# Ranking of a routed mixture: search rounds with four candidates, list slots marked and turned by small products, row maxima over 512 keys

## The reference, cut to what matters

```python
def block(q_blk):                                        # attention, 8 heads, 2560 keys for the 2048 sample queries
    s = (jnp.einsum('bqhd,bkhd->bhqk', q_blk[..., :QK_NOPE], k_nope)
         + jnp.einsum('bqhr,bkr->bhqk', q_blk[..., QK_NOPE:], kpe))
    p = jax.nn.softmax(s.astype(jnp.float32) * scale, axis=-1).astype(v.dtype)
...
cap = EC_FACTOR * n // N_EXPERTS                         # 256 of the 2048 sample tokens for each expert
aff = jax.nn.softmax((h @ w_router).astype(jnp.float32), axis=-1)
vals, idx = lax.top_k(aff.transpose(0, 2, 1), cap)
xg = jax.vmap(lambda hb, ib: hb[ib])(h, idx)
```

## Time and profile before

| | us |
|---|---|
| median of 3 runs | 3122.05 |
| lowest, highest | 3120.58, 3127.84 |
| the profiled execution | 3117.55 |
| its span in the trace | 3115.5 |

### The profile page before, as it was taken

How to read it: one execution, slowest core, us unless ns; L and a number is a source line. 1 busy time by engine, 2 the same in 40 slices (tenths; PEclk the granted TensorE clock), 3 DMA queues, 4 the chain that set the end, 5 groups by cost and what they waited for, 6 DMA issues and landing times. The chain is left out here.

```text
span 3115.5 us, 43716 instructions
## 1 busy us (share of the span) xinstructions
PE 2905.0 (93%) x16781; PEld 2331.0 (75%) x16781; DVE 2019.8 (65%) x2589; ACT 1087.0 (35%) x1722; POOL 1065.6 (34%) x686
## 2 busy tenths in 40 slices
PE   6999999999789999999999999989948999999993
PEld 3888888888667777777777767878827888888882
DVE  5418292829357888878888865555684566666655
ACT  5311111111344444444444443223413333333344
POOL 1000000000123334444334546411107666656652
PEclk8999999999889999999999999999968999999996
DMA  6213222211541110110111136575415676666667
GB/s 231 100 53 107 78 104 81 105 66 54 183 141 24 27 31 14 27 34 13 25 27 33 34 124 197 186 251 172 144 72 174 197 203 192 194 198 200 198 188 286
DMA packets 139666, 371.48 MB, mean 119 GB/s; under 512 B 20902, under 2 KB 48012, under 8 KB 129260
## 3 DMA queue, kind: packets, MB, share of 16 engines
q1 hardware_dynamic: 100028, 266.74, 25.7%
q0 software_dynamic: 23920, 74.70, 8.9%
q10 hardware_dynamic: 15552, 27.79, 2.5%
HBM read 266.25 MB, written 102.89 MB: 118 GB/s over the span
## 5 line engine op out<-in xcount | busy, mean ns | idle before, releaser
L1176 ACT ACTIVATE at_w<-banks 128x512 f32<-128x512 f32 (+1 forms) x592 | 347.6, 591 | 467.0 <-PE banks L1282 410.9
L1398 DVE TENSOR_REDUCE at_mpart<-banks 128x2 f32<-128x512 f32 x584 | 374.0, 683 | 140.1 <-PE banks L1309 139.9
L1254 POOL TENSOR_TENSOR at_part<-at_part,at_w 128x512 f32<-128x512 f32 x224 | 297.1, 1326 | 330.7 <-ACT at_w L1176 327.4
L2601 POOL TENSOR_TENSOR moe_gu_lo<-raw,moe_gu_hi 128x2048 fp32r<-128x2048 f32 x63 | 295.6, 4703 | 91.0 <-ACT moe_gu_hi L2669 90.7
L517 DVE SCALAR_TENSOR_TENSOR fr_r<-fr_r,fr_dw 128x2334 f32<-128x2334 f32 x120 | 318.0, 2650 | 3.9
L374 PE MATMUL fr_po<-hT_hi,fr_w_hi 128*128 128x512 f32 (+1 forms) x800 | 297.1, 371 | 3.1 <-PE fr_po L374 1.9
L374 PE MATMUL fr_po<-hT_hi,fr_w_lo 128*128 128x512 f32 (+1 forms) x800 | 294.7, 368 | 0.0
L374 PE MATMUL fr_po<-hT_lo,fr_w_hi 128*128 128x512 f32 (+1 forms) x800 | 294.6, 368 | 0.0
L1321 PE MATMUL banks<-at_w,V 128*64 128x256 f32 (+1 forms) x2368 | 283.0, 381 | 0.0
L2791 DVE TENSOR_TENSOR moe_d_lo<-moe_raw_d,moe_d_hi 128x1024 fp32r<-128x1024 f32 x64 | 200.7, 3136 | 102.8 <-ACT moe_d_hi L2701 97.5
L1425 DVE TENSOR_TENSOR at_part<-at_part,at_w 128x512 f32<-128x512 f32 x224 | 231.8, 1035 | 13.0
(11 more groups left out here) (406 smaller groups left out, 6833.0 us busy)
## 6 DMA issues: line engine op xcount, KB each, us to landing
raw<-w_gate_up SPq DMA_DIRECT2D x64, 1024.0 KB
moe_raw_d<-w_down SPq DMA_DIRECT2D x64, 512.0 KB
fr_wm<-w_ada_rows POOLq DMA_DIRECT2D x32, 512.0 KB, 4.6
gates_scratch<-fr_r ACTq DMA_DIRECT2D x64, 256.0 KB, 2.0
mx_gates<-gates_scratch SPq DMA_DIRECT2D x64, 256.0 KB, 3.4
fr_raw<-w_in SPq DMA_DIRECT2D x28, 512.0 KB, 5.2
fr_r<-x POOLq DMA_DIRECT2D x18, 512.0 KB, 5.6
raw<-mixed_scratch SPq DMA_DIRECT2D x9, 1024.0 KB, 6.0
```

What stands on the lines that cost most here:

```text
L1176: act.activation(w[:, g % NW, k, 0:n], sc[:, (2 * g + k) % SCB, 0:n], ACT.Exp, scale=SM_SCALE).then_inc(exp_done, 1)
L1254: pool.tensor_tensor(part[:, j % 2, 1, 0:n], before, w[:, g % NW, 1, 0:n], ALU.add).then_inc(add_p, 1)
L1398: dve.tensor_reduce(mpart[:, s, 2 * half:2 * half + 2, c], max_bank(m, half), AX.X, ALU.max).then_inc(red_done, 1)
L2601: pool.tensor_tensor(gu_lo[:, slot], raw_gu[:, slot], gu_hi[:, slot].bitcast(F32), ALU.subtract).then_inc(glo_done, 1)
```

## The change

**Attention.** For the steps that come in pairs (all but the ninth of a sample block and the prompt's), `max_products` makes two products of 128 queries by 512 keys instead of four by 256. The even step takes query tiles 0 and 1, the odd one tiles 2 and 3, each with the keys of both steps; a bank then holds one query tile. `mpart` shrinks from 9 to 5 columns.

**Search round.** There are four candidates, the first being the bits found so far, whose count is a constant 64 per row. The new `low` is the largest candidate that is reached: compare and multiply in one instruction, a maximum over four, and one instruction that joins the next bits to it. `digit`, `kept` and the separate update of `low` go.

**Tail.** Both threshold comparisons run one behind the other and one reduction counts them. DVE writes for each list its end, and a row of 256 marks in bfloat16, 1 where the slot is at or behind that end (`past`, four instructions). PE turns and sums these by small products: per quarter two slot halves, each with `stride_b` (how far the next list lies) and with `less` (minus what the list gave). `diag`, `offs`, `places`, `begins`, `begun` go. Constants: `rank_slot`, `rank_ones` and `rank_lists` give way to `rank_stride` and `rank_slots`; ACT converts the slot numbers to bfloat16 ahead of the copy that completes `listed`.

```diff
+        def paired(m):
+            _, b, c = STEPS[m]
+            return b < NB and c < NS - 1
+
+        def max_unit(m, half):
+            _, b, c = STEPS[m]
+            first = 2 * (c % 2) + half if paired(m) else 2 * half
+            tiles = 1 if paired(m) else 2
+            k0 = key_tiles(b, c - c % 2) * P
+            bank = bank_of(("unit", UNITS[m] + half)).rearrange("p (q n) -> p q n", q=tiles)
+            return bank, slice(first, first + tiles), slice(k0, k0 + BLK // tiles)
...
-                    pe.wait_ge(hi_piece, PIECES * h + (PIECES if h else pieces(b, c)))
+                    pe.wait_ge(hi_piece, PIECES * h + (PIECES if h else pieces(b, c + 1 - c % 2 if paired(m) else c)))
...
-                        for i in range(2):
-                            at = tok + (2 * half + i) * P
-                            mm = pe.matmul(max_bank(m, half)[:, i, :], q_hi[u][0:HQ, at:at + P], k_hi[u][0:HQ, k0:k0 + 256],
-                                           start=True, stop=True)
+                        bank, tiles, keys = max_unit(m, half)
+                        for i in range(tiles.stop - tiles.start):
+                            at = tok + (tiles.start + i) * P
+                            mm = pe.matmul(bank[:, i, :], q_hi[u][0:HQ, at:at + P], k_hi[u][0:HQ, keys], start=True, stop=True)
...
-                        dve.tensor_reduce(mpart[:, s, 2 * half:2 * half + 2, c], max_bank(m, half), AX.X, ALU.max
-                                          ).then_inc(red_done, 1)
+                        bank, tiles, _ = max_unit(m, half)
+                        dve.tensor_reduce(mpart[:, s, tiles, c // 2], bank, AX.X, ALU.max).then_inc(red_done, 1)
...
+                act.wait_ge(slots_ld, 16)
+                act.activation(slots_b, slots, ACT.Copy).then_inc(same_done, 1)
                 act.wait_ge(max_done, QUARTERS * LIST // 8)
                 act.activation(listed[:, :, :, 1], val[:], ACT.Copy).then_inc(listed_done, 1)
...
                     dve.wait_ge(total_done, r + 1)
-                    dve.tensor_scalar(reach[:], total, float(CAP), None, ALU.is_ge, ALU.add, accum_out=digit[:]).then_inc(digit_done, 1)
-                    dve.wait_ge(digit_done, r + 1)
-                    wait(dve, low_done, r + 1)
-                    dve.tensor_scalar(kept[:], digit[:], float(4 ** (ROUNDS - 1 - r)), None, ALU.mult).then_inc(kept_done, 1)
-                    dve.wait_ge(kept_done, r + 1)
+                    dve.scalar_tensor_tensor(out=reach[:], in0=total, scalar=float(CAP), in1=cand[:].bitcast(F32),
+                                             op0=ALU.is_ge, op1=ALU.mult).then_inc(reach_done, 1)
+                    dve.wait_ge(reach_done, r + 1)
+                    dve.tensor_reduce(low[:], reach[:], AX.X, ALU.max).then_inc(low_done, 1)
+                    dve.wait_ge(low_done, r + 1)
                     if r + 1 < ROUNDS:
-                        dve.scalar_tensor_tensor(out=cand[:], in0=bits[:, r + 1], scalar=kept[:], in1=low[:],
-                                                 op0=ALU.bitwise_or, op1=ALU.bitwise_or).then_inc(cand_done, 1)
-                        dve.wait_ge(cand_done, r + 2)
-                    dve.tensor_scalar(low[:], low[:], kept[:], None, ALU.bitwise_or).then_inc(low_done, 1)
-                dve.wait_ge(low_done, ROUNDS + 1)
+                        dve.tensor_scalar(cand[:], bits[:, r + 1], low[:].bitcast(U32), None, ALU.bitwise_or).then_inc(cand_done, 1)
...
-                for n, compare in ((n_gt, ALU.is_gt), (n_ge, ALU.is_ge)):
-                    tail_step(over[:], aff4[:], low[:, 0:1].bitcast(F32), None, compare, op=dve.tensor_scalar)
-                    with nc.allow_low_precision(reason="whole numbers up to 64 are exact in bfloat16"):
-                        tail_step(n[:], over[:], AX.X, ALU.add, op=dve.tensor_reduce)
+                for n, compare in enumerate((ALU.is_gt, ALU.is_ge)):
+                    dve.tensor_scalar(over3[:, n], aff4[:].rearrange("p q n -> p (q n)"), low[:], None, compare).then_inc(tail, 1)
+                steps_done[0] = 2
+                with nc.allow_low_precision(reason="whole numbers up to 64 are exact in bfloat16"):
+                    tail_step(n_both[:].rearrange("p c q -> p (c q)"),
+                              over3[:, 0:2].rearrange("p c (q n) -> p (c q) n", n=LIST), AX.X, ALU.add, op=dve.tensor_reduce)
...
+                tail_step(out=less[:], in0=take[:].unsqueeze(2).to_broadcast([P, QUARTERS, E]), scalar=-1.0,
+                          in1=same_b[:, 0:E].unsqueeze(1).to_broadcast([P, QUARTERS, E]), op0=ALU.mult, op1=ALU.mult,
+                          op=dve.scalar_tensor_tensor)
                 dve.wait_ge(sums_done, 2)
-                tail_step(diag, ident[:].unsqueeze(1).to_broadcast([P, QUARTERS, P]),
-                          off_sum.unsqueeze(2).to_broadcast([P, QUARTERS, P]), ALU.mult, op=dve.tensor_tensor)
+                dve.wait_ge(same_done, 4)
+                tail_step(end[:], off_sum, take[:], ALU.add, op=dve.tensor_tensor)
+                dve.wait_ge(tail, steps_done[0])
+                for q in range(QUARTERS):
+                    dve.tensor_scalar(past[:, q], slots_b, end[:, q:q + 1], None, ALU.is_ge).then_inc(tail, 1)
                 dve.wait_ge(sums_done, 3)
-                dve.wait_ge(lists_ld, 16)
-                tail_step(places, lists, offs, ALU.add, op=dve.tensor_tensor)
-                dve.wait_ge(x2_st[0], 16 * PAIRS)
-                for i in range(2):
-                    tail_step(out=begins[:, i], in0=offs.rearrange("p (g e) -> p e g", e=E), scalar=slot_of[:, i:i + 1],
-                              in1=places.rearrange("p (g e) -> p e g", e=E), op0=ALU.is_ge, op1=ALU.mult,
-                              op=dve.scalar_tensor_tensor)
-                tail_step(begun[:], begins, AX.X, ALU.max, op=dve.tensor_reduce)
-                tail_step(pos[:], begun[:], base[:], ALU.add, op=dve.tensor_tensor)
+                dve.tensor_tensor(pos[:], place, base[:], ALU.add).then_inc(tail, 1)
...
-                pe.wait_ge(tail, 9)
-                pe.matmul(offs, ones_b, diag.rearrange("p q n -> p (q n)"), start=True, stop=True).then_inc(sums_done, 1)
+                for q in range(QUARTERS):
+                    pe.wait_ge(tail, 10 + q)
+                    for i in range(2):
+                        cols = slice(i * P, (i + 1) * P)
+                        pe.matmul(place[:, i], past[:, q, cols], stride_b, start=(q == 0), stop=False, skip_group_check=True)
+                        mm = pe.matmul(place[:, i], past[:, q, cols], less[:, q], start=False, stop=(q == QUARTERS - 1),
+                                       skip_group_check=True)
+                mm.then_inc(sums_done, 1)
```

More of the change, by code:

```diff
@@ L1904, in out_phase @@
[L1904 to L1909, removed]
@@ L1910, in out_phase @@
-        spare = k.sb("spare", [P, QUARTERS])
+        cand, low = k.sb("cand", [P, 4], U32), k.sb("low", [P, 1])
+        reach = k.sb("reach", [P, 4])
+        bits = k.sb("bits", [P, ROUNDS, 4], U32)
+        same, before, stride = k.sb("same", [P, P]), k.sb("before", [P, P]), k.sb("stride", [P, E])
+        same_b, before_b = (wraw[:, 0, n * P // 2:(n + 1) * P // 2].bitcast(BF16) for n in range(2))
+        stride_b = wraw[:, 0, P:P + E // 2].bitcast(BF16)
+        slots, slots_b = wraw[:, 1, 0:CAP], wraw[:, 1, CAP:CAP + CAP // 2].bitcast(BF16)
@@ L1911, in out_phase @@
+        group0, base = k.sb("group0", [P, QUARTERS]), k.sb("base", [P, 2, E])
+        count = k.sb("count", [P, 4], BF16)
+        n_both = k.sb("n_both", [P, 2, QUARTERS], BF16)
+        n_gt, n_ge = n_both[:, 0], n_both[:, 1]
+        n_eq, take = (k.sb(n, [P, QUARTERS], BF16) for n in ("n_eq", "take"))
+        spare, end, less = k.sb("spare", [P, QUARTERS]), k.sb("end", [P, QUARTERS]), k.sb("less", [P, QUARTERS, E], BF16)
         over3 = x[:, 0, 0:3 * QUARTERS * LIST].rearrange("p (c n) -> p c n", c=3)
-        diag = x[:, 0, 3 * QUARTERS * LIST:].bitcast(BF16).rearrange("p (q n) -> p q n", q=QUARTERS)
@@ L1925, in out_phase @@
+        count_done, total_done, low_done, cand_done = (
+            k.sem(n) for n in ("count_done", "total_done", "low_done", "cand_done"))
         atp_done, turned, tab_done, tail, sums_done, listed_done, list_st = (
@@ L2039, in _ @@
                 split_m(1, 1, 0)
-                act.wait_ge(const_ld, 16 * 7)
+                act.wait_ge(const_ld, 16 * 6)
                 act.wait_ge(w_lo_done[0], 1)
-                for dst, src in ((same_b, same[:]), (before_b, before[:]), (ones_b, ones[:])):
+                for dst, src in ((same_b, same[:]), (before_b, before[:]), (stride_b, stride[:])):
                     act.activation(dst, src, ACT.Copy).then_inc(same_done, 1)
@@ L2220, in _ @@
                 dve.memset(tab[:], 0.0).then_inc(tab_done, 1)
-                dve.memset(low[:].bitcast(F32), 0.0).then_inc(low_done, 1)
-                dve.wait_ge(const_ld, 16 * 7)
```

(10 more changed lines are left out.)

48 lines of the change are left out of this document (17 added, 31 removed).

## The result

| | before | after |
|---|---|---|
| median us (lowest to highest) | 3120.58 (3119.82 to 3127.84) | 3103.62 (3100.54 to 3110.2) |
| the profiled execution | 3117.55 | 3106.41 |
| its span | 3115.5 | 3104.6 |

The ratio is 0.9947, 95% interval 0.9931 to 0.9962. The touched parts came close to what was forecast for them, 1 to 2 us over in all. The rest of the missing 7 us is in the one stage that was let pass as a block, the experts.

The account below looks back on a forecast made before the run. PE was taken to bound attention and DVE's chain of small instructions the ranking's end; 3.5 (attention) + 1.8 (search rounds) + 4.5 (tail) = 9.8 us off the median 3122.05 gave 3112.2 us, range 3107 to 3119.

Parts of the forecast that it names:

- Attention, forecast 3.5: Attention's paired steps: two 512-column products replace four of 256, saving 0.014 us in each of 248 steps; bounds 1.0 to 6.0.
- Rival 1: Attention gives only a fixed cost per matmul or nothing: 0 to 1.2 us there, 6.3 to 7.5 in all; chance 0.14.
- The forecast's own rows, 7, 18 and 27 ns: Attention: savings per paired step before a score, ahead of the values and in the other room of keys, 0.007, 0.018, 0.027 us.
- rival 4: Attention: DVE becomes the bound if a 512-element one-row reduction takes over 0.24 us more; slower, 3168 us; chance 0.04.
- Search rounds, forecast 1.8: Search in `out_phase`: 0.66 us for 0.77 in 14 rounds (1.5) plus 0.25 in the last; bounds 0.6 to 2.6.
- The hold in round 3: Search round 3: `cand`, held by POOL's addition for 2.13 us instead of 0.22, stays held; 0 gained beyond the round's share.
- rival 2: Search round 3: POOL's hold on the new `cand` goes, 1.9 us more, 11.7 in all, 3110.3 us; chance 0.10.
- Tail, forecast 4.65 us: End of `out_phase`, first threshold comparison to end of `pos`: 4.65 us for 9.12, saving 4.5; bounds 3.8 to 4.9.
- Rival 5: Tail: marks cost twice the fp32 row and products their weight loads; saves 2.0 instead of 4.5, 3114.7 us; chance 0.05.
- 6.3 forecast: Ranking in `out_phase`: search rounds (1.8 us) and tail (4.5 us) together.
- I let them shift as a whole: Experts' stage: starts by `pos`, first weights asked for inside `out_phase`, so it moves unchanged in length; nothing gained.
- The range: Whole kernel: 3107 to 3119 us, said to take in all but the slower case and spread of the median.

Follow-up runs that it names:

- after_again: The changed kernel run once more, nothing altered, for a second trace: 3101.82 us, ratio 0.9942 to the kernel before.

## Why the prediction was wrong, step by step

- **Attention, forecast 3.5: right in kind, a little small.** From the 11th to the 141st group of values products it is 780.0 to 780.2 us in all seven profiles with the old maxima and 775.5 to 776.3 in all seven with the new. That is 3.7 to 4.7 us for the 224 paired steps between them (448 products of 512 columns), 17 to 21 ns a step where 14 was taken. All 248 give 4.1 to 5.2, inside the bounds. Rival 1 is out. By the 2.5 ns a matmul of the Trainium skill, "TensorE: Matmul & The Clock Gate", section "Wait — 56ns, not 53.3ns?", it would be 1.2 us. (The forecast's own rows, 7, 18 and 27 ns, were 1.4 to 5.4 times that rule's 5, not two to five.)
- **DVE in attention (rival 4): out.** 682 ns; the idle time before the reductions was 139.0 us and is 137.7 (121.8 and 15.9 before the 71 unpaired ones).
- **Search rounds, forecast 1.8: 2.1.** 0.64 us for 0.77, 14 times (1.8), and 0.37 (2326.43 - 2326.06) for 0.64 in the last (0.27). The maximum over four takes 0.16 us, where 0.15 was taken.
- **The hold in round 3 (rival 2): stayed.** 2.14 us for 2.13, ending with POOL's addition. The Trainium skill, "SBUF — State Buffer", section "Who interferes with whom", counts `tensor_scalar` among the instructions that can contend with GpSimd, where it enters a 2-port mode; this four-word one was held.
- **Tail, forecast 4.65 us: 4.64.** The marks are 0.2 apart, and `pos` follows PE by 0.37. Rival 5 is out. Rounds and tail together, from the first comparison of the search to the end of `pos`, are 59.1 us in all six profiles with the old ranking and 52.6 in all eight with the new: 6.5 for the 6.3 forecast. (The whole stages of the first two profiles lie 9.2 us apart. The rest goes with PE's granted clock at the router's products: 0.62 in the mean from 2262 to 2271 before, part of it at the lower of its two levels (1.2 GHz), and 1.00 (2.4 GHz) after. In the 14 profiles the stage takes 231.7 to 232.3 us up to the first comparison where the clock stayed at 1.00 there, and 234.0 to 235.8 where it fell, and either ranking has both.)
- **"I let them shift as a whole": the step that failed.** The experts' stage was priced at nothing, by one argument: its weights are asked for before. Its length was named as a thing that would show the prediction wrong, and it did: 767.4 us in the mean of four profiles at the old place of DVE's instructions, 761.4 in four at the new, and 7.2 us between them where only the fourth to the sixteenth gather is counted. What the forecast missed is a wait: DVE's `moe_h_lo` is held through two POOL instructions twice in every pass of the loop before and once after. Not the data or the timing of the change did that, but its number of instructions on DVE. The forecast of 9.8 plus 6.0 to 7.2 is 15.8 to 17.0; with attention and the rounds at their measured size it is 17 to 19, where 17 was measured, and 18 by the ratio of `after_again`.
- **The range** had no room for it: all rivals but one took from the gain of the touched stages, and none changed a stage that the diff does not touch.

The trace of before had the warning in it. `moe_h_lo` took 0.42 us in three of four cases and 7.2 to 7.5 in the fourth, in every expert of the loop from the fourth on. An instruction with two lengths that is held by another engine hangs on the order of two starts, and so can tip either way by a few tenths of a microsecond.

## What to carry to other kernels

A stage that a change doesn't touch can still change its pace when its engines' streams move; look there for an instruction with two very different lengths, and put a few microseconds either way into the range. Before crediting a gain in such a stage to the change, put the lost instructions back as idle work and see whether the gain stays. Where one engine holds another across two long instructions in a row, try a wait that makes a gap between them: here 0.4 us of waiting removed 4.5 us of hold, at every second expert after and at every one before, and an expert's pace went from 43.3 to 42.9 us and from 43.9 to 43.1.

## What was new about the hardware

- An engine's own stream can pause where nothing is waited for: 0.35 us in the first pass and 0.11 in later ones, at a place that moves with the number of instructions ahead of it (47 back: the pause is back; 8 more: it is gone from that place). A packet of a DMA queue of the kind "instruction" moves with it, 0.35 to 0.61 us behind the instruction that follows the first pause.
- POOL's issue of an indirect transfer took 1.74 us instead of 0.96 when it came 0.32 us behind the start of DVE's `moe_d_lo`, a subtraction with two SBUF inputs. It ended 0.83 us after DVE did, and so it did with 1.99 us when it came 0.07 us behind. 0.04 us ahead of it, it was not held, and neither was DVE (1.23 us both times).
- DVE's `moe_h_lo` was held through two POOL instructions in a row (7.21 us), not only through the one that was running when it was issued.
